# The last expert's gate and up matrices in two halves of rows, one semaphore for each

## The reference

```
for e in range(N_EXPERTS):                      # 32
    hid = silu(h @ w_gate[e]) * (h @ w_up[e])   # w_gate, w_up: 1024 x 256
    out = out + combine[:, e:e+1] * (hid @ w_down[e])   # w_down: 256 x 1024
```

## Time and profile before

| what | value |
|---|---|
| runs of the kernel | 1070.24, 1070.86, 1073.32 us |
| median | 1070.86 us |
| span of the profiled execution, first to last instruction | 1071.4 us |
| time of the profiled execution beside its span | not given apart |
| mean granted TensorE clock | 0.927 |
| PE busy, PE weight loads busy | 920.9 us (86%), 673.7 us (63%) |
| DVE, ACT, POOL busy | 412.8 us (39%), 285.3 us (27%), 270.5 us (25%) |
| moved over the span | 277.68 MB, mean 259 GB/s |

### The profile page before, as it was taken

The page is one execution under the profiler, slowest core; times in us unless marked ns, Lnnn a source line. Parts: engine busy times, 40 slices in busy tenths (PEclk is TensorE's granted clock), DMA queues, the critical chain, the costliest instruction groups (busy, mean ns, idle before and its releaser), DMA issues. The chain is left out here.

```text
span 1071.4 us, 18728 instructions
## 1 busy us (share of the span) xinstructions
PE 920.9 (86%) x7252; PEld 673.7 (63%) x7252; DVE 412.8 (39%) x952; ACT 285.3 (27%) x591; POOL 270.5 (25%) x423
## 2 busy tenths in 40 slices
PE   6999998985998889886599999769959998797885
PEld 5888877964555555553587878458835555454553
DVE  5256773346111111111668878653462111111114
ACT  5355653231211112110442111262322111111103
POOL 0900000013343334311043525220123442342110
PEclk8999998996999989999589999989969999999998
DMA  7512110676999999994825634315869999999956
GB/s 231 176 35 59 40 42 21 232 297 243 387 416 416 419 415 413 418 421 170 284 60 138 158 87 118 86 50 190 363 230 365 413 416 418 417 414 420 420 221 249
DMA packets 111699, 277.68 MB, mean 259 GB/s; under 512 B 34888, under 2 KB 73112, under 8 KB 86986
## 3 DMA queue, kind: packets, MB, share of 16 engines
q1 hardware_dynamic: 96054, 253.74, 62.1%
q0 software_dynamic: 11424, 17.87, 4.6%
q10 hardware_dynamic: 4132, 4.86, 1.9%
HBM read 266.25 MB, written 27.45 MB: 274 GB/s over the span
## 5 line engine op out<-in xcount | busy, mean ns | idle before, releaser
L1948 DVE COPY areaB<-ps 128x512 f32<-128x512 f32 x66 | 45.7, 692 | 362.2 <-PE ps L1931 362.2
L1914 PE MATMUL ps<-ring,areaB 128*64 128x256 f32 x640 | 157.1, 402 | 25.2 <-issue 23.5
L1915 PE MATMUL ps<-ring,areaB 128*64 128x256 f32 x640 | 157.5, 403 | 0.0
L1960 POOL DMA_INDIRECT pair_rows<-areaB,idx x66 | 67.6, 1024 | 266.8 <-DVE areaB L1948 259.3
L1914 PEld LDWEIGHTS ps<-ring,areaB 128*64 128x64 f32 x640 | 89.3, 145 | 69.7 <-issue 31.1
L1939 ACT ACTIVATE v_rows<-ps 128x256 f32<-128x256 f32 x66 | 25.3, 383 | 277.4 <-PE ps L1915 277.4
L1015 PE MATMUL ps<-conv_x_high,pw_halves 128*128 128x272 f32 x512 | 90.1, 297 | 0.3 <-DVE areaS L1219 0.3
L1915 PEld LDWEIGHTS ps<-ring,areaB 128*64 128x64 f32 x640 | 89.4, 145 | 0.0
L1955 POOL DMA_INDIRECT areaC<-h_rows,idx x66 | 68.7, 1040 | 55.8 <-issue 45.3
L1936 ACT ACTIVATE areaB<-ps 128x512 f32<-128x512 f32 x66 | 39.4, 597 | 149.1 <-PE ps L1906 149.1
L1931 PE MATMUL ps<-ring,areaB 128*64 128x512 f32 x320 | 76.1, 593 | 1.6 <-DVE areaB L1945 1.6
(11 more groups left out here) (351 smaller groups left out, 1812.7 us busy)
## 6 DMA issues: line engine op xcount, KB each, us to landing
ring<-in_w_gate SPq DMA_DIRECT2D x40, 1024.0 KB, 25.9
ring<-in_w_up SPq DMA_DIRECT2D x40, 1024.0 KB, 28.2
ring<-in_w_down SPq DMA_DIRECT2D x40, 1024.0 KB, 26.8
areaA<-in_w_gate SPq DMA_DIRECT2D x12, 1024.0 KB, 21.2
areaA<-in_w_up SPq DMA_DIRECT2D x12, 1024.0 KB, 24.1
wring<-in_w_down SPq DMA_DIRECT2D x12, 1024.0 KB, 21.0
h_T<-in_w_gate SPq DMA_DIRECT2D x12, 1024.0 KB, 22.6
h_T<-in_w_up SPq DMA_DIRECT2D x12, 1024.0 KB, 25.3
```

The lines of the kernel that those rows point to most:

```text
L1914: pe.matmul(ps[0:CAP, 2 + odd, 0:F], rows, ring_gate(ws)[:, k, :], start=(k == 0), stop=(k == KT - 1))
L1915: mm = pe.matmul(ps[CAP:P, 2 + odd, 0:F], rows, ring_up(ws)[:, k, :], start=(k == 0), stop=(k == KT - 1))
L1948: return v.tensor_copy(rows_out[:, s, :], ps[:, 5 + odd, :])
L1960: return gp.indirect_dma_start(pair_half_rows, bass.IndirectOffsetOnAxis(idx[:, RING + s:RING + 1 + s], 0), rows_out[:, s, :], None, bound ...
```

## The change

The load of the last position issues four transfers of 512 KB in place of two of 1 MB: rows 8p to 8p+3 of gate, the same of up, rows 8p+4 to 8p+7 of gate, the same of up. The first two raise one new semaphore, the last two another. The products of the last tile no longer wait for the slot's semaphore ahead of step k = 0; they wait for the first new semaphore ahead of k = 0 and for the second ahead of k = 4. It applies to both layers. Nothing else is changed.

```
+            last_half_landed = [sem(f"last_half_landed{l}{a}") for a in range(2)]
...
-            def gate_and_up(pe, s, odd, ws):
+            def gate_and_up(pe, s, odd, ws, halves_landed=None):
                 for k in range(KT):
+                    if halves_landed and k % (KT // 2) == 0:
+                        pe.wait_ge(halves_landed[k // (KT // 2)], 32)
...
-                        load_gateup(sp, l, expert, position % RING)
+                        if position < NE - 1:
+                            load_gateup(sp, l, expert, position % RING)
+                        else:
+                            for a in range(2):
+                                ks = slice(a * KT // 2, (a + 1) * KT // 2)
+                                for dst, w in ((ring_gate, w_gate), (ring_up, w_up)):
+                                    src = w[l, ds(expert, 1)].rearrange("e (p k) f -> p (e k) f", p=P)[:, ks, :]
+                                    sp.dma_start(dst(position % RING)[:, ks, :], src).then_inc(last_half_landed[a], 16)
...
-                        else:
+                        elif not final:
                             pe.wait_ge(gateup_landed[l][x.ws], 32 * x.wq + 32)
                         after(pe, gateup_kept, x.e - 1)
-                        gate_and_up(pe, x.s, x.odd, x.ws).then_inc(gateup_done, 1)
+                        gate_and_up(pe, x.s, x.odd, x.ws, last_half_landed if final else None).then_inc(gateup_done, 1)
```

## The result

| | before | changed |
|---|---|---|
| median | 1070.55 us | 1065.56 us |
| lowest to highest (4 runs each) | 1069.76 to 1073.32 | 1063.55 to 1067.12 |
| ratio to before, 95% interval | | 0.9936 [0.9914, 0.9957] |
| span of the profiled execution | 1071.4 us | 1065.4 us |
| mean granted clock in it | 0.927 | 0.933 |

The medians differ by 5.0 us, the means by 5.6. The ratio says 6.9 us (of 1070.55), with 4.6 to 9.2 as its interval; why it says more than the eight runs in the table do, the record doesn't show. The forecast was 4.8 us and 1066.1 us; the ratio times 1070.55 is 1063.7 us, just under the range's low end of 1063.8.

A forecast was written before the change was run, and what follows sets the result against it. The last expert's up matrix was taken to hold up PE at each layer's end. Gains of 1.62 us (layer 1) and 3.30 us (layer 0), less 0.1, gave 4.8 us: 1070.9 to 1066.1 us, range 1063.8 to 1069.2.

The forecast's parts named there:

- What bounds the end: Last tile of each layer: PE idles 1.98 us (layer 1) and 3.29 us (layer 0) for the last expert's up matrix.
- When the halves land: Last expert's load: first half costs no wait in layer 1; second half lands as up did, 0.12 us later.
- the two bounds: First half's landing: at the latest 2.45 us before up's old landing, at the earliest where gate landed.
- The forecast 0.12 us: Delay of the second half's landing in each layer, from 4 KB pieces at 410 in place of 419 GB/s.
- The saved products: Last tile: half the products, 1.74 us, leave the path; gain 1.62 us in layer 1, 3.30 us in layer 0.
- What it adds: Two more SP issues a layer, down issued some 4 us later but covered; extra PE waits cost 0.1 us for the kernel.
- The 1.84 us of the earlier trace: A PE wait read as followed by clock 0.50, evidence that waits near 2 us go either way.
- The half clock stays in layer 0: Rival, layer 0's last tile: two waits still bring 1.2 GHz, 1.68 us not saved; 3.1 us gain, 1067.8; chance 0.14.
- A half clock is saved in layer 1 as well: Rival, layer 1: kernel before sometimes loses 1.7 us more, which the change saves; 6.5 us gain, 1064.4; chance 0.10.
- Small transfers are slower: Rival, last expert's loads: each half pays a slow begin, 1.5 us a layer; gain 2.1 us, 1068.8; chance 0.07.
- slower: Rival, both layers: halves move at 258 GB/s throughout, landing 3.1 us later; 4.5 us slower, 1075.4; chance 0.05.
- the first half is no earlier: Rival, last loads: transfers end out of order, first semaphore comes with the second; no gain, 1070.9; chance 0.06.

The follow-up runs named there:

- e4: Changed kernel with its four half transfers kept, but the last tile's products wait for both semaphores ahead of step 0; ratio 0.9999 to the kernel before.
- e2: The change (halves and their two waits) in layer 0 alone, layer 1 as before; ratio 0.9957 to the kernel before.
- e3: The change (halves and their two waits) in layer 1 alone, layer 0 as before; ratio 0.9965 to the kernel before.
- e5: Kernel before with gate and up of all 27 reloaded positions in halves, every tile still waiting for both matrices in full; ratio 1.0084, 9.0 us slower.
- e9: Kernel before, nothing split, with unread unit-matrix products filling TensorE's wait for the last expert's matrices; ratio 0.998.
- e10: Kernel before, unchanged, timed as if it were a change; ratio 0.9977.
- e7: Kernel before with whole 1 MB transfers, but the last tile runs all gate products, then all up products, each after its own semaphore; ratio 0.9992.
- e1: The changed kernel once more, no edit, timed in five rounds; ratio 0.9952 to the kernel before, median 1065.99 us.
- e11: The changed kernel a third time, no edit; ratio 0.9949 to the kernel before.

## Why the mechanism was right and the size was missed

**What bounds the end: right.** The two waits were for the up matrix. In e4 they came back with the single wait, and in e2 and e3 layer by layer.

**When the halves land: right.** The first half in layer 1 lands before TensorE is free (1024.06 against 1024.52), in layer 0 it is 0.79 us late, where at most 0.84 was forecast (491.36 - 490.52). It lands 2.43 and 2.49 us before the second half: the late one of the two bounds, 2.45 us, was the true one. Without e5, the first refill to landing took 226.65 to 228.54 us in eleven traces of layer 0, with no order by halved or whole. In layer 1 it took 227.15 to 227.43 in the three kernels made from the one before (before, e9, e10) and 228.0 to 228.42 in those made from the changed one, but e2 (228.20) and e7 (228.10) are among these, and their transfers in layer 1 are whole. So these 0.8 us are not the price of halves; what they are stays open. The forecast 0.12 us is lost in that; e5 has a rate near the one behind it. The Trainium skill (DMA: Bandwidth & Descriptors, Rules for kernel authors) asks for at least 1 MiB in a transfer for maximum bandwidth, and its section Measured has 341 GB/s for 1 MB, in transfers issued from GpSimd. By that figure the halves would have cost 1.15 us a layer, an estimate. Four queued transfers of 512 KB from SP did not show that; the 411 GB/s of e5 lies far above 341.

**The saved products: right.** Landing to pair loads fell by 3.40 us in layer 0 and 1.71 in layer 1. From the landing the forecast was 1.74 + 1.68 = 3.42 and 1.74.

**What it adds: right.** No step behind the new issues waited. Their size was short: in layer 1 down went out 11.1 us after the first gate issue in place of 4.1, so 7 us later and not 4 (5.5 us in layer 0). It landed 21.8 us after its issue, and 2.4 us before it was used.

**The size and the range: the step that failed.** The first measure says 6.9 us where the sum says 4.8, and 1063.7 us lies 0.1 us under the range. Two terms of the prediction were mis-sized: the clock in the sum, and the spread in the range.

The first is the step in which the sum of one profiled execution was set against the median: "Layer 1 ... 1.62 us", with the half clock there as a rival of 0.10, and layer 0's half clock as if it were always there. Five traces have the single wait in each layer (the kernel before or an experiment with the same order of waits):

| single wait in layer 0 | before | e3 | e4 | e5 | e10 | mean |
|---|---|---|---|---|---|---|
| wait, us | 3.29 | 3.29 | 3.42 | 3.41 | 2.29 | |
| the clock fell | yes | yes | yes | no | no | |
| landing to pair loads | 14.79 | 14.85 | 15.92 | 13.15 | 13.18 | 14.38 |

| single wait in layer 1 | before | e2 | e4 | e5 | e10 | mean |
|---|---|---|---|---|---|---|
| wait, us | 1.98 | 2.00 | 2.23 | 2.09 | 1.97 | |
| the clock fell | no | no | yes | yes | no | |
| landing to pair loads | 12.69 | 12.79 | 14.58 | 14.39 | 12.78 | 13.45 |

With two waits the stretches are 11.37 and 10.98 us. Where the clock falls, the gain is 3.4 to 4.5 us in layer 0 and 3.4 to 3.6 in layer 1; where it does not, 1.7 to 1.8 us in each. One execution can therefore gain from 3.5 to 8 us by this alone, and 4.8 was one draw, in layer 0 with the fall and in layer 1 without. The means give 3.0 us in layer 0, where 3.30 was forecast, and 2.5 in layer 1, where 1.62 was: 5.5 us. Five traces are few. Both falls in layer 1 are in e4 and e5, which split the transfers; of the three single-wait traces with whole transfers none has one, and the same sum over those three traces in each layer is 4.7 us.

The second is the spread of the rest, which I set at one fall of the clock, 1.7 us, with "some tenths" at the ends of the range. Single runs of the kernel before went from 1065.91 to 1077.48 us (one of 4412.56 left aside). In the traces the stage before the first refill ended between 260.5 and 266.7 us, and pair loads to the next refill took 292.6 to 296.0. The ratio of e10 shows what is left of this after twelve runs: 2.5 us for no change at all, and the changed kernel had four in its first measure.

All the runs on record together give the best size: 103 runs of the kernel before average 1071.44 us and 23 of the changed one (4, 10 and 9) average 1066.28. That is 5.2 us, with some 0.8 us to each side (an estimate from their scatter). The 4.8 us of the sum lie in this, the 6.9 us of the first measure do not. The three ratios of the changed kernel are 0.9936, 0.9952 and 0.9949, and the forecast's 0.9956 lies in the intervals of all three. So the larger part of the miss is the range, which was too narrow for a measurement of four runs, and the smaller part, 0.4 us, is in the sum. That the first measure was high by chance is likely, not shown.

One reading behind the clock terms was wrong as well. The 1.84 us of the earlier trace rows are a part of a wait on the chain. The timeline of PE has the whole of it:

```profile
991.94 0.40 PE L1914 MATMUL ps<-ring,areaB 128*64 128x256 f32 x1 [2.25 <-issue]
```

That waits near 2 us go either way stands all the same: the two tables have it, and in the kernel before a wait of 1.87 us at 394.95 was followed by a mean of 0.52 from 396 to 399 us.

**The rivals.** "The half clock stays in layer 0" did not happen in any of the four traces with halves in layer 0 (after, e1, e2, e11). "A half clock is saved in layer 1 as well" had its case in two of five traces with a single wait there. "Small transfers are slower" (2.1 us of gain), "slower" and "the first half is no earlier" are excluded by the ratios and the landings.

## What to carry to other kernels

When a queue of transfers is full to its end, what can be shortened is the work left behind its last landing; splitting did not move the landing itself. Let each product wait only for the piece that it needs, and split only the last load: halving all 27 cost 9 us. Cut along the contraction (the rows of the matrix), so that products that overlap stay together; cutting by matrix gave the whole gain back. And where the clock sometimes falls after a wait, size a forecast from more than one trace, and its range from repeated runs of the unchanged kernel: the same kernel has several times.

## What was not expected of the hardware

Halves of 512 KB, in pieces of 4 KB in place of 8 KB, for two thirds of the bytes cost 2% of the rate in a full queue (411 against 419 GB/s) and 9 us where all were cut. Gate and up products on the two column halves of the array took 3.48 us when they alternated and about 6 us one matrix after the other. And the same wait was followed by either clock: 3.41 us (e5) left it at 1.00 where 3.29 us (before) was followed by 0.50, and 1.98 us (before) left it at 1.00 where 2.09 us (e5) was followed by 0.51.
